# Turned feed-forward tiles: the products with high and with low weights of a bank in two groups of four instead of in turn

## The chip, the cores and the metric

One Trainium2 chip, one of its cores. The metric is the device time of one execution in microseconds (us); lower is better. The kernel before takes 1790.29 us (median of 3 runs, 1788.45 to 1790.33).

## The reference

Two blocks of two layers each over 256 tokens of width 1024, all in float32. In each layer of the first block a feed-forward part of width 2816 stands before and after an attention mixer; in each layer of the second one it stands after the mixer. So there are six feed-forward parts, and they are all alike:

```
def swiglu(x, w_gate, w_up, w_down):
    return (jax.nn.silu(x @ w_gate) * (x @ w_up)) @ w_down
```

The change touches the two products `x @ w_gate` and `x @ w_up` (in the second block they are the halves of `h @ w_ffn_in`). Everything else, the down product, the mixers and their projections, is as it was.

## The kernel before, in words

**Precision.** A float32 operand is split into a high part (rounded to the fp32r type that the matmul takes) and a low part (the rest). A product of two such operands is three matmuls that add into the same PSUM bank: high by high, high by low, low by high. ACT makes the high part of the weights (`w_hi`, L717), DVE the low part (`w_lo`, L1222), both from `raw`, into which SyncE's DMA queue puts the weights in units of 128x2048 numbers. There are four slots of each; PE waits for a unit in `split_ready` (semaphore `units_split`) and gives it back with `units_used`.

**Wide products.** Most products keep the tokens as the stationary operand and move 512 columns of weights: lines L1955, L1956 and L1957 of the helper `three`, each with its own weight load (PEld). The down products of the feed-forward parts are of this kind (with `gT_hi`, `gT_lo`), and so are the projections and the first of the eleven tiles of a feed-forward part.

**Turned tiles.** The other ten tiles of a feed-forward part (`turned_tile`) are computed the other way around: the 128x128 weights are stationary and the tokens move. `aT` holds the normalised tokens, turned, as `[128, 2, 8, 256]`: the high half (`aT_hi`) and the low half (`aT_lo`) of 256 columns each. A matmul with `w_hi` as the stationary operand moves both halves at once, 512 columns, into both halves of a bank (L2091, called H here); one with `w_lo` moves `aT_hi` alone, 256 columns, into the first half of the bank (L2092, called L here). Later ACT and DVE add the two halves of the bank. So the three matmuls are two here.

A turned tile reads two weight units (`j`), and each unit feeds four banks (`n`), with four blocks `c` for each bank: 2 x 4 x 4 = 32 pairs of H and L. The eight pairs of one bank and one unit's four blocks follow each other on PE; a unit's four pairs into one bank are called a group below. There are 8 groups in a tile, 80 in a feed-forward part, 480 in the kernel: 1920 H and 1920 L. Tile 1 and tile 2 are written out, with five small matmuls between them (L2104, L2108); tiles 3 to 10 are four rounds of a loop of two tiles.

**What sets the order.** The order on each engine is the order in which the code is written. PE computes; ACT and DVE split the weights of the units to come, and between two splits they read the finished banks: ACT at L766 after `gates_summed` (the gate banks are complete) and at L771 after `units_used` of the tile's second unit. These two semaphores are raised by the last matmul of a bank, an L, in both kernels.

Of the kernel before, what the change touches and what calls it, by code (L numbers as in the profile page):

```python
# [22 lines left out]
P = 128  # L23
# [3 lines left out]
KC = DM // P  # L27
# [73 lines left out]
def stream1(l):  # L101
    return Stream(l * U1)


def stream2(l):
    return Stream(DEPTH * U1 + l * U2)


def build(nc, I, out):
    L = DEPTH  # L110
    with ExitStack() as ctx:
        def sb(name, shape, dt=F32):
            return ctx.enter_context(nc.sbuf_tensor(name, shape, dt))
# [6 lines left out]
        w_hi = sb("w_hi", [P, SLOTS, UNIT], F32R)  # L120
        w_lo = sb("w_lo", [P, SLOTS, UNIT], F32R)
        x = sb("x", [P, 2, DM])
        xn = sb("xn", [P, 2, DM])
        aT = sb("aT", [P, 2, KC, SEQ], F32R)
        aT_hi, aT_lo = aT[:, 0], aT[:, 1]
# [1824 lines left out]
        def _(pe):  # L1950
            M = nc.tensor.matmul
# [7 lines left out]
            def split_ready(st, p, it=0):  # L1959
                pe.wait_ge(units_split, st.index(p, it) + (1 + SLOTS))  # L1960
# [8 lines left out]
            def stage(src, ready, n, i, banks=STAGE_BANKS):  # L1969

                pe.wait_ge(ready, n * 2 + (i + 1))
                turned(src, i, 0, banks)
                turned(src, i, 1, banks)

            def second_half(src, ready, n, banks=STAGE_BANKS):

                return lambda j, k: stage(src, ready, n, 1, banks) if (j, k) == (0, 2) else None

            def full_k(st, S, pt, it, banks, m, beside=None, before=None, half=None):


                for j, i in ((0, 0), (0, 1), (1, 0), (1, 1)) if S is None else ((0, 0), (1, 0), (0, 1), (1, 1)):
                    p = pt + j
                    if i == 0:
                        split_ready(st, p, it)
                    if before is not None and j == 0:
                        before(i)
                    if S is not None:

                        pe.wait_ge(stage_ready, S + (1 + 2 * i + j))  # L1990
                    for c in range(4):
                        k = 4 * j + c
                        o = three(ps[:, banks[i], 0:m], aT_hi[:, k, P * i:P * i + P], aT_lo[:, k, P * i:P * i + P],
                                  w_hi[:, st.slot(p), 512 * c:512 * c + m], w_lo[:, st.slot(p), 512 * c:512 * c + m],
                                  k == 0, k == KC - 1)
                        if i == 1 and c == 3:
                            o.then_inc(units_used, 1)
                        if half is not None and (j, i, c) == (1, 0, 3):
                            o.then_inc(half, 1)
                        if beside is not None:  # L2000
                            beside(j, 4 * i + c)
# [6 lines left out]
            def first_tile(st):  # L2008

                for n, (i, j) in enumerate(FIRST_PARTS):  # L2010
                    pe.wait_ge(stage_ready, n + 1)
                    for c in range(4):
                        if i == 0 and c == 0:
                            pe.wait_ge(half_split, j + 1)
                        if i == 0 and c == 2:
                            split_ready(st, j)
                        k = 4 * j + c
                        o = three(ps[:, i, :], aT_hi[:, k, P * i:P * i + P], aT_lo[:, k, P * i:P * i + P],
                                  w_hi[:, st.slot(j), 512 * c:512 * c + 512], w_lo[:, st.slot(j), 512 * c:512 * c + 512],
                                  k == 0, k == KC - 1)  # L2020
                        if i == 1 and c == 3:
                            o.then_inc(units_used, 1)
                        if (n, c) == (0, 0):
                            first_turned(1)
                        elif (n, c) == (0, 3):
                            first_turned(2)
                        elif (n, c) == (1, 3):
                            first_turned(3)
# [43 lines left out]
            def ffn(st, F, S, p0, X, nxt=None, banks=STAGE_BANKS, aside=None):  # L2072

                def turned_tile(t, pt, it=0):
                    b = pt // 2 - p0 // 2
                    for j in range(2):
                        p = pt + j
                        split_ready(st, p, it)  # L2080
                        if j == 0 and not (isinstance(t, int) and t < 2):
                            pe.wait_ge(g_ready, F * FT + t - 1)
                        for n in range(4):
                            if isinstance(t, int) and (t, j, n) == (2, 0, 2):
                                pe.wait_ge(gT_ready, F * FT + 1)
                            bank = TILE_BANKS[b % 2][n // 2] + n % 2
                            o = ps[:, bank, :].rearrange("p (h n) -> p h n", h=2)
                            for c in range(4):
                                k, w = 4 * j + c, 512 * c + P * n
                                wh, wl = w_hi[:, st.slot(p), w:w + P], w_lo[:, st.slot(p), w:w + P]  # L2090
                                M(o, wh, aT[:, :, k, :], start=k == 0, stop=False, skip_group_check=True)  # L2091
                                r = M(o[:, 0], wl, aT_hi[:, k, :], start=False, stop=k == KC - 1, skip_group_check=True)  # L2092
                            if (j, n) == (1, 1):
                                r.then_inc(gates_summed, 1)
                        r.then_inc(units_used, 1)

                if S == 0:
                    first_tile(st)
                    pe.wait_ge(consts_ready, 1)
                else:  # L2100
                    full_k(st, S, p0, 0, (0, 1), 512, second_half(x, x_ready, X, banks))
                turned_tile(1, p0 + 2)
                pe.wait_ge(diag_ready, F + 1)
                M(ps[:, 4, 0:SEQ], ones[:, :], rstd_diag, start=True, stop=True).then_inc(row_T, 1)  # L2104
                pe.wait_ge(g_ready, F * FT + 1)
                for c in range(2):
                    for i in range(2):
                        o = nc.tensor.transpose(ps[:, 5, SEQ * c + P * i:SEQ * c + P * i + P],  # L2108
                                                gg[:, 0, i, P * c:P * c + P], ident[:, :])
                o.then_inc(g_T, 1)  # L2110
                turned_tile(2, p0 + 4)
                with pe.Fori(0, 4) as it:
                    turned_tile(it * 2 + 3, p0 + 6, it)
                    turned_tile(it * 2 + 4, p0 + 8, it)

                pe.wait_ge(g_ready, F * FT + FT - 1)
                if aside is not None:
                    aside()
                for u in range(U_DOWN - 2):
                    pe.wait_ge(gT_ready, F * FT + u + 1)  # L2120
                    wide(st, p0 + U_UP + u, u, gT_hi, gT_lo, 2 * u, order=(1, 0) if u == 0 else (0, 1),
                         between=(lambda: pe.wait_ge(g_ready, F * FT + FT)) if u == 0 else None)
                wide_pair(st, p0 + U_UP + U_DOWN - 2, gT_hi, gT_lo, 2 * (U_DOWN - 2),
                          lambda i, d: pe.wait_ge(gT_ready, F * FT + (U_DOWN - 1 + d)) if i == 0 else None,
                          (lambda: stage(x, x_ready, nxt, 0)) if nxt is not None else None)
# [28 lines left out]
            for l in range(L):  # L2154
                st = stream1(l)
# [110 lines left out]
                for u in range(4):  # L2266
                    p = P1_CK + u
                    split_ready(st, p)
                    for c in range(4):
                        k = 4 * u + c  # L2270
                        for n, t in enumerate((kflat, vflat)):
                            w = 512 * c + 256 * n
                            a = t[:, 60 * k:60 * k + P]
                            o = ps[:, 1, 256 * n:256 * n + 256]
                            M(o, a, w_hi[:, st.slot(p), w:w + 256], start=k == 0 and n == 0, stop=False, skip_group_check=True)
                            o = M(o, a, w_lo[:, st.slot(p), w:w + 256], start=False, stop=k == 15, skip_group_check=True)
# [162 lines left out]
            for l in range(L):  # L2439
                st = stream2(l)  # L2440
# [308 lines left out]
```

## Time and profile before

| | |
|---|---|
| median of 3 runs | 1790.29 us |
| the profiled execution, its own time | 1788.07 us |
| its span, first to last instruction | 1786.4 us |
| PE busy | 1773.3 us (99%) |
| DVE busy, ACT busy | 1231.7 us (69%), 988.0 us (55%) |
| H, count and mean record | 1920, 392 ns |
| L, count and mean record | 1920, 280 ns |

The record of a matmul reaches from its start to the modelled end of its flow through the array, and the next one starts long before that end. So the records overlap, and what one product costs is not its record but the step from its start to the start of the next. That step is read from the timeline, over a long row of products: last start less first start, divided by the number of steps.

### The profile page before, as it was taken

To read this page: it belongs to the slowest core of one execution; us is meant where nothing else is said; L and a number is where in the kernel's file an instruction comes from. 1 tells how busy PE (TensorE), PEld (TensorE's weight loads), DVE (VectorE), ACT (ScalarE), POOL (GpSimd) and SP (SyncE) were. 2 spreads that over 40 slices of the span, in tenths; PEclk is the share of its full clock that TensorE was granted. 3 is DMA by queue.
4 is the path that set the end of the run, shared out by engine and by line. 5 is a ranking of instruction groups with operands and counts; after the bars stand their busy time and mean duration, and the time that the engine had idled before them with its cause. 6 is when DMAs were issued, how large, how long until landed. Compare 5 with 4: busy or idle time off the path is not lost.

```text
span 1786.4 us, 25450 instructions
## 1 busy us (share of the span) xinstructions
PE 1773.3 (99%) x9448; PEld 1479.0 (83%) x9448; DVE 1231.7 (69%) x1753; ACT 988.0 (55%) x1333; POOL 226.2 (13%) x255
## 2 busy tenths in 40 slices
PE   9999999999999999999999999999999999999999
PEld 8888877888888888877888877778888877788887
DVE  6775667677557755767776489976775599867763
ACT  6554586565445554666555476555554466645551
POOL 0000131000000000320000096200001383100000
PEclk9999999999999999999999999999999999999999
DMA  8756472555546564544665563535656544545651
GB/s 266 221 195 203 138 211 73 188 188 188 212 145 195 194 224 143 190 119 143 195 197 198 166 212 124 181 128 182 201 195 207 168 162 143 188 159 173 192 202 75
DMA packets 221517, 316.26 MB, mean 177 GB/s; under 512 B 14168, under 2 KB 162288, under 8 KB 221168
## 3 DMA queue, kind: packets, MB, share of 16 engines
q1 hardware_dynamic: 221392, 315.02, 54.1%
q8 instruction: 57, 0.93, 0.2%
q14 instruction: 36, 0.29, 0.0%
q10 hardware_dynamic: 32, 0.01, 0.0%
HBM read 313.94 MB, written 1.05 MB: 176 GB/s over the span
## 4 chain that ended last, share of the span: by engine, by line
PE 84%; DVE 9%; DVEq 3%; ACT 2%; issue 1%; ACTq 0%; POOL 0%; POOLq 0%
PE ps L2091 25%; PE ps L1955 14%; PE ps L1957 13%; PE ps L1956 13%; PE ps L2092 13%; DVE w_lo L1222 3%; PE ps L1965 1%; ACT w_hi L717 1%; PE ps L2206 1%; PE ps L2179 1%; DVEq L1706 1%; PE ps L2194 1%; DVEq L1742 1%; DVE score L1731 1%; DVE att L1755 1%
## 5 line engine op out<-in xcount | busy, mean ns | idle before, releaser
L1222 DVE TENSOR_TENSOR w_lo<-raw,w_hi 128x2048 fp32r<-128x2048 f32 (+2 forms) x296 | 674.5, 2301 | 200.9 <-ACT w_hi L717 199.2
L2091 PE MATMUL ps<-aT,w_hi 128*128 128x512 f32 x1920 | 667.9, 392 | 0.0
L717 ACT ACTIVATE w_hi<-raw 128x2048 fp32r<-128x2048 f32 (+2 forms) x296 | 551.5, 1891 | 158.9 <-PE ps L1957 155.7
L2092 PE MATMUL ps<-aT,w_lo 128*128 128x256 f32 x1920 | 537.7, 280 | 0.0
L2091 PEld LDWEIGHTS ps<-aT,w_hi 128*128 128x128 f32 x1920 | 359.2, 187 | 79.8 <-issue 0.3
L2092 PEld LDWEIGHTS ps<-aT,w_lo 128*128 128x128 f32 x1920 | 362.9, 189 | 0.2
L1955 PE MATMUL ps<-w_hi,aT 128*128 128x512 f32 (+2 forms) x768 | 309.3, 403 | 4.3 <-DVE w_lo L1222 2.8
L1957 PE MATMUL ps<-w_hi,aT 128*128 128x512 f32 (+2 forms) x768 | 295.1, 384 | 0.0
L1956 PE MATMUL ps<-w_lo,aT 128*128 128x512 f32 (+2 forms) x768 | 294.2, 383 | 0.0
L1955 PE MATMUL ps<-w_hi,gT_hi 128*128 128x512 f32 x528 | 206.0, 390 | 0.0
L1957 PE MATMUL ps<-w_hi,gT_lo 128*128 128x512 f32 x528 | 205.6, 389 | 0.0
L1956 PE MATMUL ps<-w_lo,gT_hi 128*128 128x512 f32 x528 | 205.5, 389 | 0.0
L1955 PEld LDWEIGHTS ps<-w_hi,aT 128*128 128x128 f32 x768 | 144.3, 188 | 46.1 <-issue 16.6
L1957 PEld LDWEIGHTS ps<-w_hi,aT 128*128 128x128 f32 x768 | 144.1, 188 | 29.2
L1956 PEld LDWEIGHTS ps<-w_lo,aT 128*128 128x128 f32 x768 | 144.6, 188 | 22.9
L766 ACT ACTIVATE att<-ps 128x512 f32<-128x512 f32 x60 | 35.9, 599 | 162.6 <-PE ps L2092 162.5
L1957 PEld LDWEIGHTS ps<-w_hi,gT_lo 128*128 128x128 f32 x528 | 99.1, 188 | 20.8
L1955 PEld LDWEIGHTS ps<-w_hi,gT_hi 128*128 128x128 f32 x528 | 99.1, 188 | 20.5
L1956 PEld LDWEIGHTS ps<-w_lo,gT_hi 128*128 128x128 f32 x528 | 99.1, 188 | 20.2
L1313 DVE TENSOR_TENSOR att<-ps,att 128x512 f32<-128x512 f32 x60 | 41.5, 692 | 78.6 <-ACT att L771 78.6
L768 ACT ACTIVATE att<-att 128x512 f32<-128x512 f32 x60 | 37.9, 632 | 103.8 <-DVE att L1311 103.8
L618 POOL COPY tt<-proj 128x512 f32<-128x512 f32 x4 | 4.1, 1052 | 634.3 <-DVE proj L1453 634.3
(289 smaller groups left out, 1704.0 us busy)
## 6 DMA issues: line engine op xcount, KB each, us to landing
raw<-in_w_in SPq DMA_DIRECT2D x120, 512.0 KB, 4.6
raw<-in_w_ffn_down SPq DMA_DIRECT2D x88, 512.0 KB, 4.4
raw<-in_w_ffn_in SPq DMA_DIRECT2D x88, 512.0 KB, 5.0
raw<-in_w_ffn_gate SPq DMA_DIRECT2D x86, 512.0 KB, 4.1
raw<-in_w_ffn_up SPq DMA_DIRECT2D x86, 512.0 KB, 5.1
raw<-in_w_ffn_out SPq DMA_DIRECT2D x44, 512.0 KB, 4.7
raw<-in_w_out SPq DMA_DIRECT2D x32, 512.0 KB, 4.7
raw<-in_w_ck SPq DMA_DIRECT2D x8, 512.0 KB, 3.9
```

Of the source, the lines that this page charges most:

```text
L717: nc.scalar.activation(dst, src, ACT.Copy).then_inc(units_hi, 1)
L766: nc.scalar.activation(sil[:, b % 2], ps[:, bg:bg + 2, SEQ:2 * SEQ], ACT.Copy).then_inc(gate_lo, 1)
L768: nc.scalar.activation(sil[:, b % 2], sil[:, b % 2], ACT.Silu).then_inc(silu_done, 1)
L1222: V.tensor_tensor(o, a, h, ALU.subtract).then_inc(units_split, 1)
L1313: V.tensor_tensor(gg[:, b % 2], ps[:, bu:bu + 2, 0:SEQ], gg[:, b % 2], ALU.add)
L1706: V.drain()
L1731: V.scalar_tensor_tensor(score[:, c:c + n], relu[:, h % 2, c:c + n], iw[:, i, h:h + 1], (causal if h == 0 else score)[:, c:c + n], ALU.mul ...
L1955: M(o, ah, wh, start=start, stop=False)
L1956: M(o, ah, wl, start=False, stop=False)
L1957: return M(o, al, wh, start=False, stop=stop)
L2091: M(o, wh, aT[:, :, k, :], start=k == 0, stop=False, skip_group_check=True)
L2092: r = M(o[:, 0], wl, aT_hi[:, k, :], start=False, stop=k == KC - 1, skip_group_check=True)
```

## The change

In each group the four H come first, and then the four L. Before, they came in turn: H L H L H L H L. The operands, the banks, the number of matmuls and of weight loads, the waits and the semaphore updates are the same, and the last matmul of a group is still the L of the block `c = 3`.

```diff
                             o = ps[:, bank, :].rearrange("p (h n) -> p h n", h=2)
                             for c in range(4):
                                 k, w = 4 * j + c, 512 * c + P * n
-                                wh, wl = w_hi[:, st.slot(p), w:w + P], w_lo[:, st.slot(p), w:w + P]
-                                M(o, wh, aT[:, :, k, :], start=k == 0, stop=False, skip_group_check=True)
-                                r = M(o[:, 0], wl, aT_hi[:, k, :], start=False, stop=k == KC - 1, skip_group_check=True)
+                                M(o, w_hi[:, st.slot(p), w:w + P], aT[:, :, k, :], start=k == 0, stop=False,
+                                  skip_group_check=True)
+                            for c in range(4):
+                                k, w = 4 * j + c, 512 * c + P * n
+                                r = M(o[:, 0], w_lo[:, st.slot(p), w:w + P], aT_hi[:, k, :], start=False,
+                                      stop=k == KC - 1, skip_group_check=True)
                             if (j, n) == (1, 1):
                                 r.then_inc(gates_summed, 1)
```

PE at the start of tile 1, behind the last wide products of the first tile; the kernel before (w_hi and w_lo are the stationary weights, aT the moving tokens, ps the PSUM bank):

```order
L1956 MATMUL ps<-w_lo,aT 128x512
L1957 MATMUL ps<-w_hi,aT 128x512
L2091 MATMUL ps<-aT,w_hi 128x512
L2092 MATMUL ps<-aT,w_lo 128x256
L2091 MATMUL ps<-aT,w_hi 128x512
L2092 MATMUL ps<-aT,w_lo 128x256
L2091 MATMUL ps<-aT,w_hi 128x512
L2092 MATMUL ps<-aT,w_lo 128x256
L2091 MATMUL ps<-aT,w_hi 128x512
L2092 MATMUL ps<-aT,w_lo 128x256
```

The same place in the changed kernel, where L2090 is H and L2094 is L:

```order
L1956 MATMUL ps<-w_lo,aT 128x512
L1957 MATMUL ps<-w_hi,aT 128x512
L2090 MATMUL ps<-aT,w_hi 128x512 x4
L2094 MATMUL ps<-aT,w_lo 128x256 x4
L2090 MATMUL ps<-aT,w_hi 128x512 x4
L2094 MATMUL ps<-aT,w_lo 128x256 x4
```

The eight rows of H and L before are one group, which is now two rows of four; the pair of rows behind them is the next group. A second place is the end of tile 1 and the start of tile 2 on PE, before:

```order
L2091 MATMUL ps<-aT,w_hi 128x512
L2092 MATMUL ps<-aT,w_lo 128x256
L2104 MATMUL ps<-att,ones 128x256
L2108 MATMUL ps<-ident,att 128x128 x4
L2091 MATMUL ps<-aT,w_hi 128x512
L2092 MATMUL ps<-aT,w_lo 128x256
```

and in the changed kernel:

```order
L2090 MATMUL ps<-aT,w_hi 128x512 x4
L2094 MATMUL ps<-aT,w_lo 128x256 x4
L2107 MATMUL ps<-att,ones 128x256
L2111 MATMUL ps<-ident,att 128x128 x4
L2090 MATMUL ps<-aT,w_hi 128x512 x4
L2094 MATMUL ps<-aT,w_lo 128x256 x4
```

Nothing has moved across the small matmuls between the tiles, and the other engines have their instructions in the order of before.

## Rows read from the trace of the kernel before

**Rows 1.** The page: span, engines' busy time, chain by engine and line
```profile
span 1786.4 us, 25450 instructions
PE 1773.3 (99%) x9448; PEld 1479.0 (83%) x9448; DVE 1231.7 (69%) x1753; ACT 988.0 (55%) x1333; POOL 226.2 (13%) x255
...
PE ps L2091 25%; PE ps L1955 14%; PE ps L1957 13%; PE ps L1956 13%; PE ps L2092 13%; DVE w_lo L1222 3%; PE ps L1965 1%; ACT w_hi L717 1%; PE ps L2206 1%; PE ps L2179 1%; DVEq L1706 1%; PE ps L2194 1%; DVEq L1742 1%; DVE score L1731 1%; DVE att L1755 1%
```

**Rows 2.** The page, costliest groups: busy, mean ns of one | idle before
```profile
L2091 PE MATMUL ps<-aT,w_hi 128*128 128x512 f32 x1920 | 667.9, 392 | 0.0
...
L2092 PE MATMUL ps<-aT,w_lo 128*128 128x256 f32 x1920 | 537.7, 280 | 0.0
...
L2092 PEld LDWEIGHTS ps<-aT,w_lo 128*128 128x128 f32 x1920 | 362.9, 189 | 0.2
```

**Rows 3.** Waits: who waited for what: us in total, times, longest
```profile
PE ps L1955 <- DVE w_lo L1222: 2.8, 4, 0.9
...
ACT att L766 <- PE ps L2092: 162.5, 53, 3.6
```

**Rows 4.** Windows, PE alone: busy (records x), granted clock, DMA share, GB/s
```profile
342.83:353.43 10.60, 10.60 (x62) 1.00 0.56 181
355.35:454.15 98.80, 98.80 (x572) 1.00 0.58 192
458.62:480.38 21.76, 21.76 (x97) 1.00 0.65 242
240.23:241.41 1.18, 1.18 (x12) 1.00 0.72 113
```

**Rows 5.** Timeline of PE, turned tiles 2 to 10: start us, us, instruction
```profile
355.35 0.39 PE L2091 MATMUL ps<-aT,w_hi 128*128 128x512 f32 x1
355.58 0.28 PE L2092 MATMUL ps<-aT,w_lo 128*128 128x256 f32 x1
...
454.15 0.39 PE L2091 MATMUL ps<-aT,w_hi 128*128 128x512 f32 x1
454.38 0.28 PE L2092 MATMUL ps<-aT,w_lo 128*128 128x256 f32 x1
454.50 0.39 PE L1955 MATMUL ps<-w_hi,gT_hi 128*128 128x512 f32 x1
...
455.42 0.39 PE L1956 MATMUL ps<-w_lo,gT_hi 128*128 128x512 f32 x1
```

**Rows 6.** Timeline of PE, turned tile 1 of the same feed-forward part
```profile
342.83 0.40 PE L2091 MATMUL ps<-aT,w_hi 128*128 128x512 f32 x1
343.07 0.28 PE L2092 MATMUL ps<-aT,w_lo 128*128 128x256 f32 x1
...
353.43 0.40 PE L2091 MATMUL ps<-aT,w_hi 128*128 128x512 f32 x1
```

**Rows 7.** Timeline of PE, wide products of 512 columns
```profile
458.62 0.39 PE L1955 MATMUL ps<-w_hi,gT_hi 128*128 128x512 f32 x1
...
480.38 0.39 PE L1955 MATMUL ps<-w_hi,gT_hi 128*128 128x512 f32 x1
```

**Rows 8.** Timeline of PE, products of 256 columns one behind another
```profile
240.23 0.28 PE L2276 MATMUL ps<-w_lo,kflat 128*128 128x256 f32 x1
240.35 0.28 PE L2275 MATMUL ps<-w_hi,vflat 128*128 128x256 f32 x1
...
241.41 0.28 PE L2276 MATMUL ps<-w_lo,vflat 128*128 128x256 f32 x1
```

**Rows 9.** Timeline of PE, first wide products of 512 behind ones of 280
```profile
225.21 0.39 PE L1955 MATMUL ps<-w_hi,aT 128*128 128x512 f32 x1
...
226.13 0.39 PE L1956 MATMUL ps<-w_lo,aT 128*128 128x512 f32 x1
```

**Rows 10.** Timeline of the weight loads (PEld) and matmuls in tile 4
```profile
374.42 0.19 PEld L2092 LDWEIGHTS ps<-aT,w_lo 128*128 128x128 f32 x1
374.65 0.19 PEld L2091 LDWEIGHTS ps<-aT,w_hi 128*128 128x128 f32 x1
...
374.42 0.39 PE L2091 MATMUL ps<-aT,w_hi 128*128 128x512 f32 x1
374.65 0.28 PE L2092 MATMUL ps<-aT,w_lo 128*128 128x256 f32 x1
374.77 0.39 PE L2091 MATMUL ps<-aT,w_hi 128*128 128x512 f32 x1
```

## The prediction

> **What bounds the kernel now.** I read the page first: PE is busy for 1773.3 of 1786.4 us, and the chain that ended last runs over PE's matmuls, the turned H (L2091) with 25% and the turned L (L2092) with 13% of the span [rows 1]. Then the costliest groups: no H or L ever finds PE idle (0.0 us before both of 1920) [rows 2]. Then the waits: the longest sum in which PE waits for anyone is 2.8 us, at the wide products; ACT waits for PE's L 162.5 us in total, not the other way around [rows 3]. So in the turned tiles PE sets the pace alone, and the change can gain or lose only by the steps between PE's own starts. DVE and ACT stand in the shade of it.
>
> The steps come from the timeline and the windows that count the records. From the second pair of tile 2 on (the first starts with an exposed load after the small matmuls; I leave out one more) to the last pair of tile 10 there are 98.80 us [rows 4, 5]. The window counts 572 records, two of which had started earlier; 570 products are 285 pairs, so **346.7 ns a pair**, 230 for H and 117 for L (355.35 to 355.58 is the H step) [rows 5]. In tile 1 the pair is longer: 10.60 us for 60 products (62 records, two of them from before) [rows 4, 6], **353.3 ns a pair**. The clock is granted in full (1.00) in both stretches [rows 4], so tile 1 is not slow by the clock, nor by waiting. The operands are of the same kind, and PE's program is the same; it is the entry that differs: tile 1 follows wide products without a break, tile 2 follows the small matmuls. I read this as two ways in which starts and loads can mesh, of which the trace names no cause.
>
> **The change, part by part.** It removes and adds nothing: 1920 H, 1920 L, 3840 loads before and after. No wait moves, no semaphore update moves against its group's end, no DMA is touched. What changes is which product follows which: of the eight steps of a group, four were H to L and four L to H; now three are H to H, one H to L, three L to L, one L to H (at the group's end). So the sum is: 480 groups times the new length S of a group, less the old one. The old one is 4 x 346.7 = 1386.7 ns in 432 groups (tiles 2 to 10) and 4 x 353.3 = 1413.3 in 48 groups (tile 1), in the mean 1389.4 ns.
>
> For S the trace has no row of H H H H L L L L. The nearest rows give bounds:
>
> 1. *Long rows of 512 columns.* The wide products step in 21.76 us over 96 products, 226.7 ns each (97 records, one of them from before) [rows 4, 7]. That is 3 ns under the H step of now.
> 2. *Long rows of 256 columns.* L2275 and L2276 add 256 columns into one half of a bank, each pair into the same place, each with a load of its own. From 240.23 to 241.41 there are ten steps [rows 8] (12 records in the window, with the one still running and the last) [rows 4]: 117 to 118 ns. That is the L step of now. So four short products in a row, and sums into the same place at that distance, cost nothing new.
> 3. *Entering 512 behind shorter products.* Behind products of 280 columns the first four steps of 512 take 0.92 us [rows 9], and behind the last L the first four wide steps take 0.92 us too [rows 5]: 230 ns each. A longer row then falls to 226.7; a group of four doesn't last that long.
>
> Lower bound by points 1 and 2 of this list: S = 4 x 226.7 + 4 x 117.4 = 1376.4. By 3 and 2: S = 4 x 230 + 4 x 117.4 = 1389.6. And if each product keeps the cost over its columns that it has now: one pair's 768 columns at 2.4 GHz are 320 ns, so 26.7 ns are left for two products, 13.3 each; a wide product has the same (226.7 less 213.3). By that rule (step = columns at the clock plus 13.3 ns, whatever stands beside it) the order is of no effect: **S = 1386.7**, and tile 1 has the same. I take this value: it lies between the two others and explains both of the kernel's longest steady stretches with one number. The change is then 480 x (1386.7 - 1389.4) = **-1.3 us**, all of it from tile 1.
>
> The profiled execution took 1788.07 us with a span of 1786.4, so 1.7 us lie around the span; the median of the runs is 1790.29, 2.2 us above the profiled one. I forecast against the median: 1790.29 - 1.3 = **1789.0 us**; a profiled execution like this one would have a span of 1785.1.
>
> **What a load does.** Each load starts with the product ahead of it, within 0.01 us of that start and never earlier: the load of w_lo at 374.42 with the H at 374.42, the load of w_hi at 374.65 with the L at 374.65 [rows 10]. Its record is 0.19 us, and still the next H starts 0.12 us after the L did [rows 10]. So the record of 189 ns [rows 2] is not what a load keeps the array from; a chain of them shows the same [rows 8]. After the change four loads in a row must each fit under an L of 117 ns; before, that was so for every second one.
>
> The Trainium skill, "TensorE: Matmul & The Clock Gate", section "Back-to-back issue gap", says that in a stream of loads and matmuls the load can run ahead through a reorder window, and gives 131 ns for a step of 512 columns and 81 ns for one of 128. No row here shows that: the wide products step 226.7 ns. By its other figure there, columns at 2.4 GHz plus 2.5 ns, a group would take about 1300 ns in either order, so the Trainium skill leaves the change at nothing where I leave it at -1.3 us.
>
> **The rivals.** The bound of what can be told from no change is 0.2%, 3.6 us; over 480 groups that is 7.5 ns a group. So it is faster if S is under 1381.9, and slower if it is over 1396.9.
>
> - *The steps compose (faster, chance 0.30).* H H H H goes at the pace of the long wide rows and L L L L at that of the chain [rows 8]. S = 1376.4, 480 x (1376.4 - 1389.4) = -6.2 us: 1784.1. For it: now H and L in turn cost 346.7, 2.6 ns more than 226.7 + 117.4, as if the turn itself cost something, and three of four turns go away. Against it: the first wide products behind shorter ones show that a row of 512 does not begin at 226.7 but at 230 [rows 5, 9].
> - *The meshing of tile 1 everywhere (slower, chance 0.18).* Each group now breaks the steady step twice, and the way of stepping is set at the entry. If PE falls into tile 1's way in all groups, S = 1413.3 and the change is 480 x 23.9 = +11.5 us: 1801.8. It decides from a third of that on (S over 1396.9). For it: the same program took 346.7 and 353.3 ns a pair [rows 5, 6], so such a state exists and it can hold for 30 pairs. Against it: in tiles 2 to 10 nothing brings it back, 285 pairs long, even over the loop's rounds and the waits for units.
> - *Loads run ahead (faster, chance 0.03).* With four long H in a row the loads of the L could be taken early, and the L would go at their columns' share of an H: 226.7/2 = 113.3. S = 4 x 226.7 + 4 x 113.3 = 1360, -14.1 us: 1776.2. Against it: no load starts before the product ahead of it does [rows 10].
> - *The loads bound the L (slower, chance 0.02).* If in a chain a load did take the time of its record, S = 4 x 226.7 + 4 x 189 = 1662.8, +131 us: 1921. The chain of 256-column products nearly excludes it [rows 8].
>
> For the rival with loads that run ahead speaks the Trainium skill ("TensorE: Matmul & The Clock Gate", "Back-to-back issue gap"), where the window pulls a load forward; the trace disagrees, since every load stands with the product ahead of it [rows 10].
>
> The forecast (S from 1381.9 to 1396.9, with the 1389.6 of point 3 in it, which gives +0.1 us) keeps 0.47; its own range is 1786.7 to 1793.9.
>
> **How the numbers follow.** Faster 0.30 + 0.03 = 0.33, same 0.47, slower 0.20. The range takes in the composed case, 1784.1, with half a microsecond of scatter, and from the slower case the part up to about half of its price: 1783.5 to 1797. Left out are the loads that run ahead and half of the slower cases and little more, under 2 in 10.
>
> **What would show it.** In the profile of the changed kernel the timeline of tiles 2 to 10 gives S directly: the start of the first H of a group to that of the next group's first H, 1.387 us. The forecast wants that within 7 ns; rivals show 1.376, 1.413, 1.360 or 1.66 there. Tile 1 should take the same S as the others; if it still takes longer, the gain of 1.3 us is gone. The loads should start with the products ahead of them as before, the waits of PE should stay at some 3 us in their longest sum, and the clock at 1.00. What would make it wrong is a step of H inside a group that is neither 227 nor 230, or a way of stepping in groups of eight that costs more than its parts; no row of before has that pattern.

## The result, and the profile after

The changed kernel takes **1794.91 us** (median of 6 runs, 1794.59 to 1796.79), the kernel before, measured beside it, 1788.49 us (median of 6, 1788.1 to 1790.33). The ratio is 1.0035, with a 95% interval from 1.0025 to 1.0045: **slower by 0.35%**, 6.4 us. That is on the slower side of the 0.2% bound, where the prediction had put 0.20, and 5.9 us above the forecast of 1789.0. It lies inside the numbers of the range, but the forecast was "no change" (a gain of 1.3 us), and that was wrong. Executions of one and the same kernel fall into two groups some 2 us apart (the kernel before 1788.1 to 1788.5 and 1790.3, the changed one 1794.6 to 1794.9 and 1796.8), so 2 us between single runs, or between medians from different groups, say nothing.

From the page of the changed kernel, its head and two of its groups:

```profile
span 1793.2 us, 25450 instructions
...
PE 1780.1 (99%) x9448; PEld 1480.9 (83%) x9448; DVE 1232.2 (69%) x1753; ACT 988.2 (55%) x1333; POOL 226.1 (13%) x255
...
L2090 PE MATMUL ps<-aT,w_hi 128*128 128x512 f32 x1920 | 524.6, 395 | 0.0
...
L2094 PE MATMUL ps<-aT,w_lo 128*128 128x256 f32 x1920 | 305.4, 281 | 0.0
```

The span grew by 6.8 us (from 1786.4 [rows 1]), and so did PE's busy time; DVE and ACT moved by half a microsecond or less. The busy time of H *fell*, from 667.9 [rows 2] to 524.6 us, and that of L from 537.7 to 305.4. That says nothing on speed: busy time is the union of a group's records, and four H in a row overlap each other, where in turn they overlapped with the L, which are another group. The mean records (395 and 281 ns against 392 and 280) hardly tell either. Only steps do.

The waits of PE in the changed kernel (total, times, longest), and the one of ACT for L:

```profile
PE ps L1955 <- DVE w_lo L1222: 2.9, 4, 0.9
...
ACT att L766 <- PE ps L2094: 168.7, 53, 3.7
```

PE waits for nobody more than before (2.8 and 162.5 us in [rows 3]); ACT waits for PE 6 us more. So the time went into the steps of PE, and the prediction's two last signs of being wrong are to be looked for there: an H step that is neither 227 nor 230 ns, and a way of stepping in groups of eight that costs more than its parts. The loads did not change their place: all but eight of the 3840 loads of H and L start within 5 ns after the start of the matmul ahead, as before. Windows over the turned tiles of part 2 (busy, records, clock, DMA share, GB/s):

```profile
357.42:455.64 98.22, 98.22 (x562) 1.00 0.57 189
345.31:353.73 8.42, 8.42 (x50) 1.00 0.44 145
```

and the timeline of PE in one group and the start of the next (start, length of the merged rows):

```profile
375.65 1.09 PE L2090 MATMUL ps<-aT,w_hi 128*128 128x512 f32 x4
376.58 0.63 PE L2094 MATMUL ps<-aT,w_lo 128*128 128x256 f32 x4
377.05 1.09 PE L2090 MATMUL ps<-aT,w_hi 128*128 128x512 f32 x4
377.98 0.64 PE L2094 MATMUL ps<-aT,w_lo 128*128 128x256 f32 x4
378.46 0.40 PE L2090 MATMUL ps<-aT,w_hi 128*128 128x512 f32 x1
```

Between 357.42 and 455.64 lie 560 products (562 records, two from before), 70 groups: **S = 98.22 / 70 = 1403.1 ns** (from unrounded starts 1403.2, and 1403.3 over whole weight units, since groups of 1401 and of 1405 to 1406 ns alternate). From 345.31 to 353.73, in tile 1, there are six groups (48 products): 1403.3 ns. Both windows begin and end at an H that opens a group. The single group takes 375.65 to 377.05, 1.40 us: four H in 0.93 us (232 ns each), four L in 0.47 us (118 each). So tiles 2 to 10 lost 16.6 ns a group (from 1386.7 to 1403.3), tile 1 gained 10 (from 1413.3): 432 x 16.6 = 7.2, less 48 x 10 = 0.5, is +6.7 us of the span's +6.8. The clock stayed at 1.00. Below, S is always the mean of many groups in the steady part of a stretch, from the start of the first H of a weight unit (or of a group) to the start of such an H later on.

### The profile page after: what moved, and what is told of

Its sections match the earlier page's. It is cut to its first block, busy times and chain, and to the rows that moved or that the text cites. A ratio compares the mean times of both kernels' runs of the same rounds, so it can differ in the third digit from the quotient of the medians.

```text
span 1793.2 us, 25450 instructions
## 1 busy us (share of the span) xinstructions
PE 1780.1 (99%) x9448; PEld 1480.9 (83%) x9448; DVE 1232.2 (69%) x1753; ACT 988.2 (55%) x1333; POOL 226.1 (13%) x255
## 4 chain that ended last, share of the span: by engine, by line
PE 83%; DVE 10%; DVEq 3%; ACT 2%; issue 1%; ACTq 0%; DMA 0%; POOL 0%; SPq 0%
PE ps L2090 25%; PE ps L1955 14%; PE ps L1957 13%; PE ps L1956 13%; PE ps L2094 13%; DVE w_lo L1222 4%; PE ps L1965 1%; ACT w_hi L717 1%; PE ps L2209 1%; PE ps L2182 1%; DVEq L1706 1%; PE ps L2197 1%; DVEq L1742 1%; DVE score L1731 1%; DVE att L1755 1%
## 5 line engine op out<-in xcount | busy, mean ns | idle before, releaser
L2090 PE MATMUL ps<-aT,w_hi 128*128 128x512 f32 x1920 | 524.6, 395 | 0.0
L2090 PEld LDWEIGHTS ps<-aT,w_hi 128*128 128x128 f32 x1920 | 328.4, 189 | 44.8 <-issue 0.3
L2094 PEld LDWEIGHTS ps<-aT,w_lo 128*128 128x128 f32 x1920 | 294.6, 189 | 40.9
L2094 PE MATMUL ps<-aT,w_lo 128*128 128x256 f32 x1920 | 305.4, 281 | 0.0
L1955 PEld LDWEIGHTS ps<-w_hi,aT 128*128 128x128 f32 x768 | 144.3, 188 | 46.1 <-issue 16.6
```

The source lines that it names most:

```text
L1955: M(o, ah, wh, start=start, stop=False)
L2090: M(o, w_hi[:, st.slot(p), w:w + P], aT[:, :, k, :], start=k == 0, stop=False, skip_group_check=True)
L2094: r = M(o[:, 0], w_lo[:, st.slot(p), w:w + P], aT_hi[:, k, :], start=False, stop=k == KC - 1, skip_group_check=True)
```

## The experiments

"Part" is one of the six feed-forward parts. The four kernels of the first table were timed on one chip with the same runs of before, and so were the four of the section behind it; each kernel with openings had a chip and runs of before of its own.

**Row length and banks.** Three theories were put up. A: a 512 step settles only in a longer row, and each change of width restarts that. B: what costs is that a product adds into the place into which its neighbour has just added. C: a fixed price on each row of H and L. The edit sets the order in which the products of a unit are written, here in short; that order is a list of (kind, bank `n`, block `c`), kind 0 for H and 1 for L:

```diff
-for n in range(4): four H of bank n, then four L of bank n
+e1_16:    [(kind, n, c) for kind in range(2) for n in range(4) for c in range(4)]
+e2_8:     [(kind, 2 * m + n, c) for m in range(2) for kind in range(2) for n in range(2) for c in range(4)]
+e3_2:     [(kind, n, 2 * m + c) for n in range(4) for m in range(2) for kind in range(2) for c in range(2)]
+e4_banks: [(kind, n, c) for c in range(4) for kind in range(2) for n in range(4)]
```

> Groups of sixteen: per weight unit all sixteen H (four banks) come first, then the sixteen L; the same products, loads and waits as the changed kernel, and only 2 changes of width per 32 products instead of 8. S is the time of 4 H and 4 L in steady tiles (before 1386.7 ns, changed 1403.3). Theory A (a step of 512 settles to 227 ns only in a longer row of equal steps, and every change of width restarts that): S about 1390, total +0.3 us against before, so 1788.8. Theory B (what costs is that L follows L, or H follows H, into the same place of the same bank): most neighbours are still in one bank, S stays at 1400 to 1406, total about +6 us. Theory C (a fixed price of 16.6 ns for each row of H and row of L): 4.2 ns a group, S 1391, not told from A here.

> Groups of eight: the H of two banks, then the L of two banks. Theory A: S between the other two, about 1395 (the eight first steps of a row of 512 behind a short one took 37 ns more than eight settled ones). Theory B: 1400 to 1406. Theory C: 1395.

> Groups of two: H H L L H H L L. Theory A: no row is long enough to settle, S as in the changed kernel or a little above, 1403 to 1410, total +6 to +10 us against before. Theory B: half of the neighbours share the place that three quarters did, S 1397 or less, total +4 us. Theory C (the price stands on each row of H and L): twice the price, S 1420, total +14 us.

> The widths come as in the changed kernel (H H H H L L L L), but the four of a row go to the four banks (block c outside, bank n inside), so no product adds into the bank that its neighbour adds into. Theory A and C: S stays at 1403, total +6.4 us against before. Theory B: S falls to 1387 or below, total 0 or a gain.

| order | S in tiles 2 to 10 (ns) | span (us) | time, ratio to before |
|---|---|---|---|
| in turn (before) | 1386.7 | 1786.4 | |
| rows of 2 (e3_2) | 1393.3 | 1790.4 | 1790.16, 1.0002 [0.9992, 1.0011] |
| rows of 4 (the change) | 1403.3 | 1793.2 | 1794.91, 1.0035 [1.0025, 1.0045] |
| rows of 8 (e2_8) | 1396.7 | 1790.3 | 1792.03, one run |
| rows of 16 (e1_16) | 1391.7 | 1797.2 | 1798.54, 1.0048 [1.0031, 1.0064] |
| rows of 4 over four banks (e4_banks) | 1403.3 | 1817.2 | 1820.35, 1.0173 [1.0156, 1.019] |

The spans are those of the profiled executions, the times medians of all runs. The kernel before, timed beside the four experiments, took 1790.0 us (13 runs, 1787.91 to 1791.98), against 1788.49 beside the changed kernel; that is why the ratios of e1_16 and e4_banks are smaller than their spans say. The profiled execution of e3_2 took 1792.1 us, 1.9 above that kernel's median. Its S and its tile 1 account for 2.0 of the 4.0 us in its span; the other 2 lie in one place, behind a wait of PE for w_lo of 2.30 us (in the kernel before the longest is 0.9 us), where the granted clock fell to 0.50 (1.2 GHz) and seven wide products stepped 427 ns each.

**B fell**: in e4_banks no neighbours share a bank, and S is that of the changed kernel; rows of 8 and 16 are below the 1400 to 1406 of B too. Rows of 8 and 16 came out as A and C said. Neither said rows of 2: A wanted 1403 or more, C 1420, and it was 1393.3, which of the three figures only B's (1397 or less) allowed. The price is not fixed on a row; it is built up over the row's first steps. The timeline of e1_16 shows it. Rows of one form are merged, and each row is read from a window that starts later than the one before, so that it begins in the middle of a run (x counts what lies in the window):

```profile
401.64 3.82 PE L2090 MATMUL ps<-aT,w_hi 128*128 128x512 f32 x16
...
402.80 2.65 PE L2090 MATMUL ps<-aT,w_hi 128*128 128x512 f32 x11
405.29 1.96 PE L2093 MATMUL ps<-aT,w_lo 128*128 128x256 f32 x15
...
405.41 1.84 PE L2093 MATMUL ps<-aT,w_lo 128*128 128x256 f32 x14
...
407.21 0.40 PE L2090 MATMUL ps<-aT,w_hi 128*128 128x512 f32 x1
```

The first five H of the row take 401.64 to 402.80, 232 ns each; the other eleven 402.80 to 405.29, 226.5 each. The first L step is 0.12 us (405.29 to 405.41; to the nanosecond in the trace 113), the following fifteen 1.80 us, 120.0 each. So a long row settles, H at 226.7 and L at **120**, and the sum of that is 4 x 226.7 + 4 x 120 = 1386.7 again. What remains is the entry: 27 ns too many over the first five H, 7 ns too few on the first L, some 20 ns for each pair of rows. With four H in a row PE pays nearly all of it (16.6 ns) in every group; with 8 it pays 20 every second group, with 16 every fourth. With 2 it pays 3.3 for each half group.

The totals of e1_16 and e4_banks (for which only +6.4 us had been expected) show something else, which S does not: their banks are finished later, and others wait. PE's waits in e1_16:

```profile
PE ps L1955 <- DVE att L1316: 7.0, 6, 1.2
PE ps L1955 <- DVE w_lo L1222: 2.9, 4, 0.9
```

and in e4_banks:

```profile
PE ps L1955 <- DVE att L1316: 11.3, 6, 1.9
PE ps L2090 <- DVE gT_lo L1336: 6.0, 6, 1.3
```

The gate banks of a tile's second unit are whole only when the L of the row have come (e1_16), or near the end of the unit (e4_banks), so ACT and DVE start on the last tile of each part late, and the down products wait for them, six times. One such wait in e1_16, and one in e4_banks with what follows it:

```profile
646.04 0.39 PE L1957 MATMUL ps<-w_hi,gT_lo 128*128 128x512 f32 x1
647.62 0.50 PE L1955 MATMUL ps<-w_hi,gT_hi 128*128 128x512 f32 x1 [1.19 <-DVE att L1316]
647.95 0.39 PE L1956 MATMUL ps<-w_lo,gT_hi 128*128 128x512 f32 x1
...
655.78 0.50 PE L1955 MATMUL ps<-w_hi,gT_hi 128*128 128x512 f32 x1 [1.91 <-DVE att L1316]
...
656.66 0.63 PE L1955 MATMUL ps<-w_hi,gT_hi 128*128 128x512 f32 x1
657.09 0.63 PE L1956 MATMUL ps<-w_lo,gT_hi 128*128 128x512 f32 x1
...
656.66:659.65 2.99, 2.99 (x9) 0.50 0.00 0
```

The idle time (7.0 us in e1_16) is less than such waits cost, because the record of the product ahead runs on into them. From start to start the step over the wait is 1.58 us in place of 0.23, and the next one 0.33: 1.46 us more, and six times that is the 8.8 us that e1_16 lost behind its turned tiles. The turned tiles themselves are 1.5 us longer and the stretch ahead of the first of them 0.6, which makes the 10.8. In e4_banks the same account gives six times 2.17 = 13.0 us for this wait, and 14.3 in the turned tiles (6.7 by S and tile 1, the rest at the wait for gT_lo). Another 3.3 us come from the clock: behind two of the six waits it fell to 0.50 (1.2 GHz), and PE stepped seven times 427 ns in place of 227; behind the four others, of the same length, it stayed at 1.00. The changed kernel has neither these waits nor this fall.

**Width, weights, the first product, and a mixture.** e7_wide_l takes the change of width away and leaves the order. e5_same_weights takes the change of weight tensor away (its L read w_hi as well, so it leaves the low part of the weights out). e9_l_first turns each pair round. e8_half mixes both orders.

The edits, shortened (e9_l_first against the kernel before, the others against the changed one):

```diff
-r = M(o[:, 0], w_lo[:, st.slot(p), w:w + P], aT_hi[:, k, :], ...)
+e7_wide_l:       r = M(o, w_lo[:, st.slot(p), w:w + P], aT[:, :, k, :], ...)
+e5_same_weights: r = M(o[:, 0], w_hi[:, st.slot(p), w:w + P], aT_hi[:, k, :], ...)
+e9_l_first:      [(1 - kind, n, c) for n in range(4) for c in range(4) for kind in range(2)]
+e8_half:         unit j == 0: four H, four L per bank; unit j == 1: H and L in turn
```

> The changed kernel, but each L moves both halves of aT too, 512 columns into the whole bank; this adds the product of low by low, which the reference's split leaves out. The order H H H H L L L L, the banks, the weights and the loads stay, only the change of width is gone. Theory A (the change of width is what unsettles PE): every step is 226.7 ns, S = 8 x 226.7 = 1813 ns. A rival by which it is the change from w_hi to w_lo weights or the two-piece moving operand of H: the first steps of each row stay long, S 1830 to 1850.

> The changed kernel, but the L take their weights from w_hi as well, so the low part of the weights is left out of the product in the turned tiles. Widths and order stay. Theory A: S 1403 as in the changed kernel, total +6.4 us. Rival (where the weights are read from matters): S moves by more than 3 ns.

> The kernel before with each pair turned round: L H L H L H L H, the bank's first product being an L. Theory A: in tiles 2 to 10 the alternation has the same step, S 1386.7. What tile 1 does is open: if its 1413.3 belongs to the way of entry (an H of 512 first behind wide products of 512), an L as the first product may bring 1386.7 there too, a gain of 1.3 us in total; if it belongs to the place, it stays.

> The first weight unit of each turned tile has the order of the changed kernel, the second one the order of before. Theory A: the first units take 4 x 1403 ns, and the second ones settle at 4 x 1386.7 within a pair or two, so 8 groups take 11.16 us in place of 11.09, and the total is +3.3 us less 0.6 in tile 1. Rival (an alternation entered behind L L L L stays in tile 1's way, 1413.3): the second units take 4 x 1413 ns, 11.27 us a tile, the total is +8 us, more than with all groups changed.

- **e7_wide_l**: S = 1813.3 ns in tiles 2 to 10 of all parts and in tile 1 of parts 2 to 6, 226.7 for each of the eight; 1991.81 us. Two weight tensors, one bank, two-piece moving operand, rows of four: none of it costs anything once the widths are equal. The change of width is what unsettles PE. (e7_wide_l also gives L the two-piece operand of H and the whole bank, so by itself it does not part the width from the form of the operand. Two other places do. In the changed kernel four H open tile 1 behind wide products of the same width but of another form, and take 343.93 to 344.84, 227 ns each: no price. And behind products of 280 columns, wide products of the same line and form do pay, as the rows under point 3 below show.) The timeline, with four H behind L of the same width, shows 0.68 us for the three L (226.7 each):

```profile
400.65 0.84 PE L2094 MATMUL ps<-aT,w_lo 128*128 128x512 f32 x3
401.33 1.07 PE L2090 MATMUL ps<-aT,w_hi 128*128 128x512 f32 x4
```

  and the place in the changed kernel:

```profile
343.71 0.39 PE L1957 MATMUL ps<-w_hi,aT 128*128 128x512 f32 x1
343.93 1.07 PE L2090 MATMUL ps<-aT,w_hi 128*128 128x512 f32 x4
344.84 0.64 PE L2094 MATMUL ps<-aT,w_lo 128*128 128x256 f32 x4
```

- **e5_same_weights**: S = 1403.3, as in the changed kernel. The weights' place does not matter. Its one time, 1797.13, is 2.2 us above the changed kernel's median; as in e3_2, 2.1 us of that lie in one place, at a wait for w_lo of 2.30 us and seven steps of 427 ns soon behind it.
- **e9_l_first**: S = 1386.7 in tiles 2 to 10 and 1413.3 in tile 1, as before, in all six parts; 1788.3 us, ratio 0.9998 [0.9988, 1.0008]. The order within the pair is of no effect, and it does not mend tile 1.
- **e8_half**: here theory A failed and its rival held. Half of the change cost more than all of it: span 1795.2 us, 2 us over the changed kernel. The mean S of tiles 2 to 10 is 1408.3; no wait or clock accounts for the difference. The units in turn do not go back to 1386.7 behind L L L L, they fall into the way of stepping that tile 1 had:

```profile
409.26 0.40 PE L2091 MATMUL ps<-aT,w_hi 128*128 128x512 f32 x1
409.50 0.28 PE L2094 MATMUL ps<-aT,w_lo 128*128 128x256 f32 x1
409.62 0.40 PE L2091 MATMUL ps<-aT,w_hi 128*128 128x512 f32 x1
409.86 0.28 PE L2094 MATMUL ps<-aT,w_lo 128*128 128x256 f32 x1
409.98 0.40 PE L2091 MATMUL ps<-aT,w_hi 128*128 128x512 f32 x1
410.21 0.28 PE L2094 MATMUL ps<-aT,w_lo 128*128 128x256 f32 x1
410.32 0.40 PE L2091 MATMUL ps<-aT,w_hi 128*128 128x512 f32 x1
```

Three pairs take 1.06 us (409.26 to 410.32), 353.3 each, over and over; H takes 0.24, 0.24 and 0.23. In tile 1 of parts 2 to 6, however, the second unit did fall into 346.7 (in part 1 into 353.3). So the alternation has **two steady paces**, and which one holds depends on how it is entered. The faster one comes in two patterns: in the kernel before, tiles 2 to 10 step 230 and 117 ns over and over; tile 1 of part 5 in e10_openings steps 231, 112, 233, 117. Both make 346.7 a pair.

**Openings.** That was tried by itself: the order of before everywhere, but for a few rows at the start of tile 1 (e10_openings), or of tiles 1 and 2 (e11_openings2), another set in each part.

```diff
-order = [(kind, n, c) for n, c in pairs for kind in range(2)]
+# rows: (2,) is H H L L and then in turn; (2, 2) is H H L L H H L L and then in turn, ...
+for m in rows:
+    order += [(kind, *p) for kind in range(2) for p in pairs[at:at + m]]
+    at += m
+order += [(kind, *p) for p in pairs[at:] for kind in range(2)]
```

> The order of before (H and L in turn) everywhere but at the very start of tile 1, where each feed-forward part opens in another way, and then goes on in turn: parts 1 and 2 with H H L L, part 3 with H H H L L L, part 4 with H H H H L L L L, part 5 with H H L L H H L L, part 6 with the L one step late through the whole first unit (H H L H L ... H L L). If which of the two ways of stepping holds is set by the phase in which the alternation is entered, some of these openings bring 1386.7 ns a group in tile 1 and some leave 1413.3. If the place sets it (its weights, its part of the program), tile 1 stays at 1413.3 in all six. Total within 2 us of before either way.

> The order of before but for the openings of tiles 1 and 2. Tile 1 opens with H H L L in part 1 and with H H L L H H L L in parts 2 to 6 (which brought it to 1386.7 ns a group in part 5 of the last experiment, and put tiles 2 to 10 into the slow way behind it). Tile 2 opens as before in part 1, with H H L L in part 2, H H L L H H L L in part 3, H H H L L L in part 4, H H H H L L L L in part 5 and H L H H L L in part 6. If the way of stepping is set anew by each entry and its phase, the same opening gives tile 1 1386.7 in all of parts 2 to 6, and some openings of tile 2 give 1386.7 in tiles 2 to 10 and others 1413.3 (101.8 us in place of 99.9 for the nine tiles). If it were the place or the loop, all parts would be alike. Total: +1.9 us for each part in the slow way, less 0.2 for each tile 1 in the fast one.

| part | e10: tile 1 opens | tile 1 | tiles 2-10 | e11: tiles 1, 2 open | tile 1 | tiles 2-10 |
|---|---|---|---|---|---|---|
| 1 | (2) | 1386.7 | 1386.7 | (2), none | 1386.7 | 1413.3 |
| 2 | (2) | 1413.3 | 1413.3 | (2,2), (2) | 1386.7 | 1413.2 |
| 3 | (3) | 1413.3 | 1386.7 | (2,2), (2,2) | 1386.7 | 1413.3 |
| 4 | (4) | 1413.5 | 1386.7 | (2,2), (3) | 1386.7 | 1386.7 |
| 5 | (2,2) | 1386.7 | 1413.3 | (2,2), (4) | 1386.7 | 1413.2 |
| 6 | L one late | 1413.3, then 1386.7 | 1413.3 | (2,2), (1,2) | 1386.7 | 1386.7 |

S in ns, of the steady part. In part 6 of e10_openings the two units of tile 1 differ: the first alternates at 353.3 ns a pair and the second at 346.7. Windows in e10_openings over tile 1 and tiles 2 to 10 of part 2, then of part 3, and last of the kernel before over tiles 2 to 10 of part 2:

```profile
342.76:353.94 11.18, 11.18 (x65) 1.00 0.58 183
354.84:456.56 101.72, 101.72 (x578) 1.00 0.57 191
529.20:540.36 11.16, 11.16 (x64) 1.00 0.59 183
541.27:641.08 99.81, 99.81 (x578) 1.00 0.59 192
...
354.57:454.38 99.81, 99.81 (x578) 1.00 0.58 194
```

All windows over tiles 2 to 10 hold the same work. Part 2 of e10_openings differs from part 2 of the kernel before in nothing but the first four products of tile 1 (H H L L in place of H L H L), and that cost 1.91 us in the nine tiles behind it (101.72 against 99.81), over five small matmuls, a loop and 285 pairs (in one profile of each kernel; the five parts 2 to 6 of before all agree). The total was expected within 2 us of before; with three parts in the slow way it came out at 1795.28 us against 1790.4, one run each. The spans agree: e11 has four stretches in the slow way, 4 x 1.91 us, less 0.2 for each of six tiles 1, +6.5 us, and its span is 1792.8 (1786.4 before); e10 has three, +5.3, and a wait for DVE's w_lo that was 1.9 us longer, and its span is 1793.6.

In parts 2 to 6 the place explains none of it: with the same opening all of them had 1386.7 in tile 1 in e11, where before they all had 1413.3. Part 1 is another matter: it had the same order in both kernels, and its tiles 2 to 10 took 1386.7 in e10 and 1413.3 in e11. So there the order alone does not decide.

**The best pair of openings.** Parts 2 to 6 got (2,2) in tile 1 and (3) in tile 2.

> The order of before, and in parts 2 to 6 tile 1 opens with H H L L H H L L and tile 2 with H H H L L L; part 1 is as before. In the last experiment this pair of openings gave 1386.7 ns a group in both stretches of part 4 (11.095 us for tile 1 in place of 11.290, 99.93 us for tiles 2 to 10). If the way of stepping is set by the entry alone, all five parts do so, and the total is 5 x 0.195 = 1.0 us under before: 1787.3 against 1788.3 or so, ratio 0.9995, which the timing may not tell from no change. If the openings worked in part 4 by chance of the place, some parts show 101.8 us for tiles 2 to 10, +1.9 us each.

Windows over tile 1 and tiles 2 to 10 of part 2 in e12_best:

```profile
344.59:355.57 10.98, 10.98 (x65) 1.00 0.57 178
356.47:456.28 99.81, 99.81 (x578) 1.00 0.58 194
```

All five parts have 1386.7 in both stretches; the same windows of before are 11.18 and 99.81 us. With the last product's step that is 0.195 us a part, 1.0 us in all. The time does not tell it from no change: 1788.73 us (11 runs) against 1789.79 (15 runs), ratio 0.9996 [0.9987, 1.0005]. Its fastest runs (1787.03 to 1787.15) lie some 0.8 us under the fastest of before (1787.93), which agrees with the 1.0 but does not prove it. Part 1, whose order is that of before, had the two ways the other way round in this profile: 1386.7 in tile 1 and 1413.3 in tiles 2 to 10 (101.85 us for the nine tiles, against 99.93 in the profile of before). The step into its first H was 320 ns here and 329 in the profile of before, after steps of 227 in both. So a few nanoseconds at the entry go with another way; that they are the cause is argued, not shown.

## Why the prediction was wrong, by its own steps

- *Only PE's steps count; nothing is added, no wait moves, the clock stays, each load stays with the product ahead of it.* Right: +6.7 of the +6.8 us are steps; the waits, the clock and the loads are those of before.
- *Tile 1 takes the same S as the others.* Right: 1403.3 in both. The gain there was 10 ns a group, not 26.6.
- *Point 1, 512 in long rows at 226.7.* Right as a steady value (e1_16, e7_wide_l).
- *Point 2, "four short products in a row cost nothing new", at 117.4.* That price came from a row that was not settled: its ten steps are between 114 and 119 ns. In e1_16 a settled L step is 120.0; in the changed kernel the mean over tiles 2 to 10 is 118.5, 1.1 ns above the term, 4 ns a group.
- *Point 3, entry at 230.* The right mechanism, mis-sized: the mean H step over the same tiles is 232.3, 9 ns a group more. Together the two give the difference between 1389.6 and 1403.2. The full price of an entry stood in the trace of before, just behind the four steps that point 3 read:

```profile
226.36 0.40 PE L1957 MATMUL ps<-w_hi,aT 128*128 128x512 f32 x1
226.59 0.39 PE L1955 MATMUL ps<-w_hi,aT 128*128 128x512 f32 x1
226.82 0.39 PE L1956 MATMUL ps<-w_lo,aT 128*128 128x512 f32 x1
227.05 0.39 PE L1957 MATMUL ps<-w_hi,aT 128*128 128x512 f32 x1
```

  From 225.21 [rows 9] to 226.82 there are seven steps in 1.61 us, 230 ns each, and only then come those of 227: together 26 ns over seven settled ones, where e1_16 has 27 over its first five. Here the row of H is entered out of its own L row, and the price falls on fewer steps.
- ***"I take this value"*: columns at the clock plus 13.3 ns, so the order is of no effect, S = 1386.7.** This is the step that failed. The rule itself holds: it gives 226.7 and 120.0, and settled rows show both. It is a rule for the steady state only, and rows of four are never in it. I had the entry's cost beside it in point 3, and the sentence that a group of four does not last long enough to settle, and gave the value without it.
- *The rival "the meshing of tile 1 everywhere" (0.18).* It named the side and the point from which it decides ("each group now breaks the steady step twice"); S went 14 of its 24 ns. But rows of four have a way of their own, 1403, in all twelve stretches of the changed kernel (tile 1 of part 1 in e4_banks, and the row-of-four unit there in e8_half, took 1400.0). The rival's own state, 1413.3, came out where H and L go in turn: in e8_half, e10, e11 and part 1 of e12. Its argument against itself, that nothing brings tiles 2 to 10 back to it, held only for the opening that the kernel happens to have.
- *The other rivals.* The steps compose, 1376.4: excluded; loads that run ahead: no step near 113 in a row's steady part; loads that bound the L: no, 120.

The Trainium skill ("TensorE: Matmul & The Clock Gate", "Back-to-back issue gap") gives columns at 2.4 GHz plus 2.5 ns as the gap of an isolated matmul. By that figure 512 columns would take an estimated 215.8 ns and 256 columns 109.2. Here no step of 512 settled under 226.7 ns, and 256 columns settled at 120.0, with a load for each product. The traces agree with the skill in that the surplus is the same for both widths, but it is 13.3 ns.

What stays open: why PE takes five steps to settle behind a change of width, what the two ways of the alternation are inside the engine, and what picks one of them in part 1, where the same order had both. The records of the loads show no difference that would name it, and no run here looked deeper.

## What to carry to other kernels

A stream of matmuls in which the width changes has a step of its own, which the settled steps of its parts do not add up to. Find the pattern's own step before grouping, or count an entry price (here some 20 ns for a pair of rows, most of it paid within five products). Per four H and four L, strict alternation paid nothing in its better way (26.6 ns in the other), rows of two 6.6, of four 16.6, of eight 10 and of sixteen 5; and the longer rows finish their results later. Where a steady stretch differs from another with the same instructions, look at how each is entered; a difference of 2% in a stretch may hang on four instructions ahead of it. And read matmuls by the step from start to start: here the busy time of H was 143 us lower in the slower order.

## What the runs showed of the hardware that was not expected

- A product with its load settles at its columns at 2.4 GHz plus 13.3 ns: 226.7 ns for 512 columns, 120.0 for 256, and 346.7 for one of each in turn.
- Rows of equal width need about five products to settle behind a change from 256 to 512 (232 ns a step, then 226.7).
- H and L in turn have two steady paces, 346.7 and 353.3 ns a pair, both stable over 285 pairs, loop rounds and semaphores on which PE did not have to stand. In parts 2 to 6 the order at the entry chooses, and over five small matmuls the opening of tile 1 still acts on tile 2 (part 2 of e10_openings against part 2 of before). In part 1, entered behind a wait, the same order had either.
- Behind a wait of 1.91 us in e4_banks and of 2.30 us in e3_2 the granted clock fell to 0.50 for a short stretch, and a step of 512 columns took 427 ns. It did not fall behind four other waits of the same length in e4_banks, nor behind one of 2.31 us in e10_openings.
- The kernel before has the good way in tiles 2 to 10 of all six parts in its profile. Nothing in its code says so, and each part that loses it costs 1.9 us.
